# Gate chunks of the filler matmuls as seven block products (Strassen's scheme on 2x2 blocks), with the block sums on GpSimd

## The reference, cut to what matters

```
h = adaLN(RMSNorm(x))
(qa, ka, va, qb, kb, vb, zb, ab, bb, qc, kc, vc, ga, gb, gc) = split_cols(h @ w_in)
merged = sigmoid(ga) * (oa @ w_br_a) + sigmoid(gb) * (ob @ w_br_b) + sigmoid(gc) * (oc @ w_br_c)
x = x + gt1 * (merged @ w_out)
x = x + gt2 * expert_choice_ffn(adaLN(RMSNorm(x)))
```

## Time and profile before

| what | value |
|---|---|
| median of 3 runs | 3084.47 us (3082.32 to 3089.09) |
| the profiled execution's own time | 3082.67 us |
| span in the profile | 3080.9 us |
| TensorE busy | 3016.1 us, 98% of the span |
| VectorE, ScalarE, GpSimd busy | 1239.3, 605.8, 233.9 us |
| weights and stores moved | 695.55 MB |

### The profile page before, as it was taken

The page is one execution under the profiler, slowest core; times in us unless marked ns, Lnnn a source line. Parts: engine busy times, 40 slices in busy tenths (PEclk is TensorE's granted clock), DMA queues, the critical chain, the costliest instruction groups (busy, mean ns, idle before and its releaser), DMA issues.

```text
span 3080.9 us, 49607 instructions
## 1 busy us (share of the span) xinstructions
PE 3016.1 (98%) x21914; PEld 1605.2 (52%) x21914; DVE 1239.3 (40%) x2404; ACT 605.8 (20%) x1349; POOL 233.9 (8%) x374
## 2 busy tenths in 40 slices
PE   7999999999999999999999999999999999999998
PEld 3555565656556444444455546666565464444443
DVE  4459553364354121221254694533644342122113
ACT  3241001144423000000032400011534230000001
POOL 0011000021001000000100100000110010000000
PEclk9999999999999999999999999999999999999999
DMA  7235442432343999999941552434224349999997
GB/s 273 93 132 194 150 150 93 146 116 74 133 157 126 386 396 400 404 396 399 378 188 55 184 197 97 151 117 145 93 74 146 141 158 408 397 404 396 397 403 285
DMA packets 102294, 695.55 MB, mean 226 GB/s; under 512 B 11786, under 2 KB 25142, under 8 KB 66752
## 3 DMA queue, kind: packets, MB, share of 16 engines
q1 hardware_dynamic: 75296, 613.97, 50.6%
q0 software_dynamic: 20736, 62.80, 7.1%
q10 hardware_dynamic: 6048, 15.62, 1.3%
HBM read 618.66 MB, written 73.68 MB: 225 GB/s over the span
## 4 chain that ended last, share of the span: by engine, by line
PE 85%; DMA 11%; ACT 2%; DVE 1%; issue 0%; DVEq 0%; ACTq 0%
PE unit L997 14%; PE unit L951 12%; PE unit L1525 11%; DMA xT<-in_w_e_gate 9%; PE work L1528 8%; PE work L1525 5%; PE unit L1009 4%; PE unit L988 4%; PE unit L1028 4%; PE unit L1381 4%; PE unit L941 3%; PE work L965 1%; PE work L1171 1%; PE work L1194 1%; PE unit L1025 1%; PE unit L1393 1%
## 5 line engine op out<-in xcount | busy, mean ns | idle before, releaser
L997 PE MATMUL unit<-hT,ring 128*128 128x512 f32 x1024 | 452.6, 594 | 0.0
L997 PEld LDWEIGHTS unit<-hT,ring 128*128 128x128 f32 x1024 | 189.4, 190 | 217.7 <-issue 217.7
L2558 DVE SCALAR_TENSOR_TENSOR arena<-work,arena 32x256 f32<-32x256 f32 x128 | 61.7, 482 | 543.1 <-PE work L1528 541.7
L1525 PE MATMUL unit<-ring,arena 128*32 128x512 f32 x2112 | 238.8, 592 | 1.3 <-DVE arena L2546 1.3
L951 PE MATMUL unit<-hT,ring 128*128 128x512 f32 x512 | 222.2, 592 | 0.0
L1528 PE MATMUL work<-ring,arena 128*32 128x256 f32 x3072 | 183.8, 380 | 0.4 <-DVE arena L2546 0.4
L2028 ACT ACTIVATE arena<-work 128x512 f32<-128x512 f32 x32 | 19.1, 597 | 821.3 <-PE work L1543 821.3
L1635 ACT ACTIVATE xT<-unit 128x512 f32<-128x512 f32 x92 | 54.8, 596 | 590.6 <-PE unit L997 384.8
L951 PE MATMUL unit<-arena,ring 128*128 128x512 f32 x384 | 167.9, 593 | 1.6 <-ACT arena L1635 0.9
L951 PEld LDWEIGHTS unit<-hT,ring 128*128 128x128 f32 x512 | 96.2, 190 | 115.8 <-issue 115.5
L1528 PEld LDWEIGHTS work<-ring,arena 128*32 128x32 f32 x3072 | 97.3, 110 | 90.4 <-issue 37.8
(11 more groups left out here) (450 smaller groups left out, 4212.5 us busy)
## 6 DMA issues: line engine op xcount, KB each, us to landing
ring<-in_w_e_up SPq DMA_DIRECT2D x64, 2048.0 KB, 25.0
ring<-in_w_in SPq DMA_DIRECT2D x32, 2048.0 KB, 12.6
arena<-in_w_e_gate SPq DMA_DIRECT2D x32, 2048.0 KB, 24.4
arena<-in_w_e_down SPq DMA_DIRECT2D x32, 2048.0 KB, 26.0
xT<-in_w_e_gate SPq DMA_DIRECT2D x30, 2048.0 KB, 26.0
ring<-in_w_e_down SPq DMA_DIRECT2D x30, 2048.0 KB, 26.4
ring<-in_w_ada SPq DMA_DIRECT2D x24, 2048.0 KB, 9.5
spill<-xT SPq DMA_DIRECT2D x94, 256.0 KB, 9.6
```

The source lines that it names most:

```text
L997: last = mm(bank[:, :], w[:, k, m * P:(m + 1) * P], hT[:, k, 0:TS], start=k == 0, stop=k == KD - 1)
L1525: last = mm(big[SLOTP * c:SLOTP * c + SLOTP, :], x[:, s0:s0 + SLOTP], w[:, kk, 512 * (c // 2):512 * (c // 2) + 512], start=k == 0, stop=k ...
L2558: STT(y[SLS:SLS + SLOTP, 256 * c:256 * c + 256], W[5][r, 0:256], gpro[r, e:e + 1], gatep[r, :], ALU.mult, ALU.mult)
```

## The change

The four gate chunks of each layer are no longer computed as 5 units. Each is cut into two pairs; pair g covers output tiles m and m + 2 of 128 columns each (m = g mod 2), the contraction is cut into two halves of 4 k-tiles, and the 640 tokens into two halves of 320. That makes a product of 2x2 blocks, and it is done in Winograd's form of Strassen's scheme: seven block products r = 0 to 6 of 4 matmuls of 128x320 each instead of eight. The block sums are 15 additions: S1 to S4 of weights (4 per pair, 128x512), T1 to T4 of h (once per layer, 128x1280), and U2, U3, C11, C12 (two steps), C22, C21 of results (7 per pair, 128x320). GpSimd does all of them (`fast_sums`), in the order of `TASKS`, interleaved by hand with its DMA issues. S3, S4 overwrite the weights in the ring, and T1 overwrites a part of hT, which is saved to DRAM (`h_spill`) at the layer's start and brought back before attention. T2 to T4 take ring slot 2, so the gate chunks use slots 1, 0, 1, 0. ACT copies each product out of PSUM (`copy_fast`), and SP stores a finished pair (`store_pair`).

The order of the fills changes too: kc moves behind ka, ada 8 and 9 stand together, ada 10 and 11 stand together, and the steps of a group have 8, 7, 7, 7, 8, 8 calls. A call is now a credit: a matmul of 128x320 costs 5 of 8.

```
-UNITS_OF = dict(ada=0, fm=5, tm=5, br=5, late=0)
+UNITS_OF = dict(ada=0, fm=5, tm=5, br=5, late=0, fast=14)
 LATE = [("gc", 0), ("gc", 1)]
 BRANCHES = "bca"
-FILL = []
-_a = 4
-for _s in [("va", 0), ("kc", 0), ("qc", 0), ("vc", 0), ("qa", 0), ("ka", 0)] + [("g" + b, i) for b in "ab" for i in (0, 1)]:
-    if _a < 12:
-        FILL += [("ada", _a), _s] + [("fold", _a)] * (_a % 4 == 3)
-        _a += 1
-    else:
-        FILL += [_s]
+FAST = [("ga", 0), ("ga", 1), ("gb", 0), ("gb", 1)]
+FILL = [("ada", 4), ("va", 0), ("ada", 5), ("qc", 0), ("ada", 6), ("vc", 0), ("ada", 7), ("fold", 7), ("qa", 0), ("ada", 8),
+        ("ada", 9), ("ka", 0), ("ada", 10), ("ada", 11), ("kc", 0), ("fold", 11)] + FAST
 SPILLED = [_f for _f in FILL if _f[0] not in ("ada", "fold")]
+PLAIN = [_f for _f in SPILLED if _f not in FAST]
...
-MSLOTS = (0, 3, 1, 2, 4, 5)
+FIRST_FAST = PLAN.index(FAST[0])
+FIRST_LATE = PLAN.index(LATE[0])
+PRE_SLOTS = [q % RING for q in range(FIRST_FAST + 1)] + [0, 1, 0, 1, 2] + [q % RING for q in range(PRE_CHUNKS - FIRST_LATE - 2)]
+SUMS_SLOT = 2
+assert PRE_SLOTS[FIRST_FAST - 1:FIRST_FAST + 1] == [0, 1] and len(PRE_SLOTS) == PRE_CHUNKS
+MSLOTS = (2, 3, 0, 1, 4, 5)
 MRING = len(MSLOTS)
-assert PRE_CHUNKS % RING == 0 and NMOE % MRING == 0
+assert NMOE % MRING == 0
...
-STEPS = (9, 8, 8, 8, 8, 8)
+STEPS = (8, 7, 7, 7, 8, 8)
 GAPS = {("kv", 3): 3, ("kv", 4): 3} | {("pp", _t): 11 for _t in range(5)} | {"inverse": 90}
 GAPS |= {(_i, _j): _q for _i in range(5) for _j, _q in enumerate(STEPS)}
 GAPS |= {("o", _h): 8 if _h == 4 else 3 for _h in (4, 0, 1, 2, 3)}
 
 
+PIECE = dict(fast=5)
...
+        elif kind_of(name) == "fast":
+            units += [(name, i, j, 4, 5) for j in range(14)]
...
+def fast_tasks(units):
+    out = []
+    for name, i, j in units:
+        if (name, i) == PLAIN[-1] and j == 2:
+            out += [("t3", 0), ("t2", 0), ("t4", 0), ("s1", 0), ("s2", 0), ("s3", 0)]
+        if (name, i) == PLAIN[-1] and j == 4:
+            out += [("t1", 0)]
+        if kind_of(name) == "fast":
+            g, r = 2 * FAST.index((name, i)) + j // 7, j % 7
+            if r == 1:
+                out += [("s4", g)]
+            if r == 2:
+                out += [("u2", g), ("c11", g)]
+            if r == 3 and g + 1 < NPAIRS:
+                out += [("s1", g + 1), ("s2", g + 1), ("s3", g + 1)]
+            if r == 4:
+                out += [("u3", g)]
+            if r == 5:
+                out += [("c12a", g), ("c12", g), ("c22", g)]
+            if r == 6:
+                out += [("c21", g)]
+    return out
...
+        sets = [xflat[:, 4 * TH * i:4 * TH * i + 4 * TH] for i in range(2)]
+        tu2, tu3 = [xflat[:, 8 * TH + TH * i:8 * TH + TH * i + TH] for i in range(2)]
+        tp2 = xflat[:, 512 * 8 - TH:512 * 8]
+        S1 = rot.rearrange("p (k m) -> p k m", k=4)
+        S2 = xflat[:, 512 * 7 - TH:512 * 8 - TH].rearrange("p (k m) -> p k m", k=4)
+        T2, T3, T4 = [ring[SUMS_SLOT][:, 4 * TH * i:4 * TH * i + 4 * TH].rearrange("p (k t) -> p k t", k=4) for i in range(3)]
+        B11, B12 = [hT[:, 0:4, TH * i:TH * i + TH] for i in range(2)]
+        B21, B22 = [hT[:, 4:8, TH * i:TH * i + TH] for i in range(2)]
...
+                def store_pair(g):
+                    name, i = FAST[g // 2]
+                    to = spill[l, SPILLED.index((name, i))].rearrange("p (h t) -> p h t", h=H)
+                    sp.wait_ge(sig["summed"], task_done(l, "c21", g))
+                    sp.dma_start(to[:, g % 2:H:2, :], sets[g % 2].rearrange("p (a t) -> p a t", a=2))\
+                        .then_inc(sig[f"stage{g % 2}_stored"], 16)
...
+                sp.wait_ge(sig["h_ready"], (l + 1) * 2 * KD)
+                hsave = hspill[l].rearrange("p (k t) -> p k t", k=4)
+                sp.dma_start(hsave, B12).then_inc(sig["x_moved"], 16)
                 last = PLAN.index(SPILLED[-1])
-                for q in range(8, last + 3):
+                for q in range(8, FIRST_FAST + 1):
                     load_plan(q)
                     store_plan(q - 3)
+                store_plan(FIRST_FAST - 1)
+                load_plan(FIRST_FAST + 1)
+                for g in range(2 * len(FAST) - 2):
+                    if g % 2:
+                        load_plan(FIRST_FAST + 2 + g // 2)
+                    store_pair(g)
...
-                store_plan(last)
+                store_pair(NPAIRS - 2)
+                sp.wait_ge(sig["unit_computed"], fast_unit(l, NPAIRS - 1, 3) + 1)
+                sp.dma_start(B12, hsave).then_inc(sig["h_restored"], 16)
+                load_plan(FIRST_LATE + 1)
+                store_pair(NPAIRS - 1)
...
+                        if kind == "t3":
+                            pool.wait_ge(sig["h_ready"], 2 * KD * (l + 1))
+                            name, value = chunk_used(chunk_no(l, "ada", 11))
+                            pool.wait_ge(sig[name], value)
+                            add(T3, B22, B12, ALU.subtract, kind)
+                        elif kind == "t2":
+                            add(T2, T3, B11, ALU.add, kind)
+                        elif kind == "t4":
+                            add(T4, B21, T2, ALU.subtract, kind)
+                        elif kind == "t1":
+                            pool.wait_ge(sig["unit_computed"], unit_no(l, *PLAIN[-1]) + 5)
+                            pool.wait_ge(sig["x_moved"], 16 * (3 * l + 2))
+                            add(B12, B12, B11, ALU.subtract, kind)
+                        elif kind == "s1":
+                            pool.wait_ge(sig[f"chunk{slot}_loaded"], 16 * n)
+                            if g:
+                                pool.wait_ge(sig["unit_computed"], fast_unit(l, g - 1, 3) + 1)
+                            else:
+                                pool.wait_ge(sig["rotated"], len(ROTATED) * (l + 1))
+                            add(S1, A21, A22, ALU.add, kind)
+                        elif kind == "s2":
+                            if g:
+                                pool.wait_ge(sig["unit_computed"], fast_unit(l, g - 1, 2) + 1)
+                            else:
+                                pool.wait_ge(sig["rotated_stored"], 16 * len(ROTATED) * (l + 1))
+                            add(S2, S1, A11, ALU.subtract, kind)
+                        elif kind == "s3":
+                            add(A21, A11, A21, ALU.subtract, kind)
+                        elif kind == "s4":
+                            pool.wait_ge(sig["unit_computed"], fast_unit(l, g, 1) + 1)
+                            add(A12, A12, S2, ALU.subtract, kind)
+                        elif kind == "u2":
+                            pool.wait_ge(sig["unit_emptied"], fast_unit(l, g, 2) + 1)
+                            add(tu2, tu2, out[:, 0:TH], ALU.add, kind)
+                        elif kind == "c11":
+                            add(out[:, 0:TH], out[:, 0:TH], tp2, ALU.add, kind)
+                        elif kind == "u3":
+                            pool.wait_ge(sig["unit_emptied"], fast_unit(l, g, 4) + 1)
+                            add(tu3, tu3, tu2, ALU.add, kind)
+                        elif kind == "c12a":
+                            pool.wait_ge(sig["unit_emptied"], fast_unit(l, g, 5) + 1)
+                            add(out[:, TH:2 * TH], out[:, TH:2 * TH], tu2, ALU.add, kind)
+                        elif kind == "c12":
+                            add(out[:, TH:2 * TH], out[:, TH:2 * TH], out[:, 3 * TH:], ALU.add, kind)
+                        elif kind == "c22":
+                            add(out[:, 3 * TH:], out[:, 3 * TH:], tu3, ALU.add, kind)
+                        elif kind == "c21":
+                            pool.wait_ge(sig["unit_emptied"], fast_unit(l, g, 6) + 1)
+                            add(out[:, 2 * TH:3 * TH], out[:, 2 * TH:3 * TH], tu3, ALU.add, kind)
...
+            def fill_fast(l, name, i):
+                w = chunk_in(chunk_no(l, name, i))
+                for j in range(2):
+                    g = 2 * FAST.index((name, i)) + j
+                    A11, A12 = w[:, 0:4, tile_t(j)], w[:, 4:8, tile_t(j)]
+                    A21, A22 = w[:, 0:4, tile_t(j + 2)], w[:, 4:8, tile_t(j + 2)]
+                    for r, (x, y, need) in enumerate((
+                            (A11, B11, None), (A12, B21, None), (S2, T2, "s2"), (S1, B12, "s1"), (A21, T3, "s3"), (A12, B22, "s4"),
+                            (A22, T4, None))):
+                        n = unit_no(l, name, i, 7 * j + r)
+                        bank = begin(n)
+                        if need:
+                            pe.wait_ge(sig["summed"], task_done(l, need, g))
+                        if g == 0 and r == 3:
+                            pe.wait_ge(sig["summed"], task_done(l, "t1", 0))
+                        for k in range(4):
+                            last = mm(bank[:, 0:TH], x[:, k, :], y[:, k, :], start=k == 0, stop=k == 3)
+                            if k == 3:
+                                used(last)
```

(82 more changed lines are left out.)

89 lines of the change are left out of this document (58 added, 31 removed).

## The result

The change makes the kernel slower: 3101.14 us median (3099.79 to 3102.31, 5 runs) against 3085.96 us (3082.32 to 3089.09, 5 runs) of the kernel before, a ratio of 1.005 with a 95% interval of 1.0039 to 1.0062. The forecast was 3077 us with a range up to 3091, so the time lies outside the range and on the other side. The profiled execution took 3101.41 us, 18.7 us more than that of before (3082.67).

What follows compares the result with a forecast made beforehand. TensorE, busy 98%, was taken to bound the kernel. Matmuls -34.6, load waits +20.2 and low clock +6.6 sum to -7.8 us, from a median of 3084.47 to 3076.7, taken as 3077 us; range 3066 to 3091.

Steps and rivals of the forecast that it cites:

- What is removed, what is put in its place: Gate chunks: 276.9 us of matmuls replaced by 448 of 128x320 at 540.8 ns, 242.3 us; gain 34.6 us.
- Loads that the new order brings close: TensorE waits 4.5 us at ka and 5.5 at kc in each layer for their loads, 20.2 us in all.
- the four parallels: Four earlier ada loads with another load 2 us behind, landing after 9.0, 9.5, 8.7 and 9.4 us, mean 9.15.
- The clock after a wait: Clock falls to half after each of four load waits, 1.64 us each, 6.6 us in all; bounds 0 and 13.
- VectorE, and GpSimd's sums at nothing: DeltaNet groups: margins of about 4 us cover GpSimd's sums and VectorE's chain, so both cost nothing.
- The rest, at nothing: h_spill, attention's value load (about 2 us later), next layer's first ada load and ScalarE's copies all cost nothing.
- rival 2: Waits at ka and kc, but full clock after them: 3070 us; chance 14%.
- Rival 4: GpSimd's sums late, by themselves or by contention with VectorE: 4 to 12 us over the forecast, 3081 to 3089; 15%.
- Rival 3: ka's and kc's loads slowed by those issued behind them, landing after 13.6 us: +10.0, 3094 us; chance 8%.

Runs made afterwards that it cites:

- small sums in the mended kernel: Changed kernel with spread fill order, values loaded first, sums behind normalization and fold 7 apart, plus each GpSimd sum cut to one column: 3054.3 us, against 3055.19 with full sums.
- by the two runs: Changed kernel with each GpSimd sum on one column: 3095.95 us; changed kernel with four stage-end sums waiting for VectorE's normalization: 3093.64 us.
- by the run: Changed kernel with the value load issued ahead of gc's second chunk load and the last pair's store: 3092.03 us, 9.1 less than the change.

## Why the prediction was wrong, by its steps

**What is removed, what is put in its place: right.** 538 ns a matmul against 541 taken from the line; gain 35.7 against 34.6.

**Loads that the new order brings close: right in place, 2.4 us small.** 22.6 us against 20.2, at ka and kc in both layers. ka waits 5.1 to 5.3 us against 4.5, kc 6.0 to 6.1 against 5.5, the landings (9.7 and 9.6 us in layer 0, 9.5 and 9.5 in layer 1) being 0.3 to 0.5 us over the 9.15 that was taken. The trace of the kernel before holds two such ada loads that were not among the four parallels: issued at 229.88 and 348.46, with another load 3 to 4 us behind, they landed after 10.0 and 9.8 us. The run without the two loads and the run of the order alone both show this mechanism.

**The clock after a wait: right in kind, mis-sized.** 6.6 us were set for the four load waits; the stretches give 10.0. The price of a wait of 1 us was taken for one of 5 or 6. Here it was 1.8 to 3.1 us, so a wait cost nearly half again its length. It also fell behind waits that the prediction did not have (3.4). The Trainium skill (TensorE: Matmul & The Clock Gate, "What's actually happening") has the throttled clock as the default state, which activity releases. All four load waits agree with it; two waits of 2.8 us had the full clock behind them, so that sentence alone does not say which waits pay.

**VectorE, and GpSimd's sums at nothing: failed at one place.** The prediction costed contention in the gaps of the groups, found 4 us of margin there, and was right there: small sums in the mended kernel gain nothing. It did not look at the end of the stage, where TensorE stands still until VectorE's five products are done and where four sums fall at the same moment. 5.6 us of waits, and 5.2 to 7.5 by the two runs. The Trainium skill (GPSIMD Engine Reference, "Key points") says that GpSimd contends with VectorE instructions that have two SBUF inputs. VectorE's products here are of that kind, and the trace agrees: 0.62 us alone, 1.15 beside the sums.

**The rest, at nothing: failed.** The sentence "the value load of attention is now behind the last pair's store: about 2 us later than before" counted the store and left out the other thing the same queue had been given ahead of it, the 2 MB load of gc's second chunk. The values came 14.1 us after their issue, where the kernel before had them in under 7; 7.0 us of waits, 9.1 by the run. The next layer's first ada load was in time, as forecast (issued 18.5 us before its use, landed 4.7 before it).

So the terms that were set at nothing (5.6 + 7.0 + 3.4 = 16.0 us) are most of the error of 26.5 on the profiled execution (+18.7 against -7.8); the clock behind the loads gives 3.4, the loads 2.4, the matmuls -1.1, and the end of the experts -0.3. The other 6.1 us lie, as far as the rows show, where the change adds and moves no work, at a lower clock: the first projection of layer 0 ends 1.0 us later, that of layer 1 begins with 32 matmuls in 10.25 us against 8.85, and around the routers the mean clock is 0.93 (960 to 1012) and 0.91 (2495 to 2575) against 0.97 and 0.98 in the same work before. The number of falls there also differs between kernels that are alike there, and no run isolates it: what these 6.1 us come from stays open.

One slip in the prediction's range changes nothing: its low end of 3066 is said to be rival 2 with the better price of the matmuls, which gives 3068; 3066 needs the better landings too.

Rival 4 named the contention but at another place. Rival 3 had the sign and came nearest (3094), 7 us low, but by luck: its mechanism did not occur, since it needs landings of 12.8 us or more and ka's and kc's loads landed after 9.5 to 9.7.

## What to carry to other kernels

An order of work that makes room for something (here two chunks at the end, so that a slot is free for sums) is to be costed for every load in it: how long is what lies between the release of its slot and its use, against the landing time; the cure was another order, not a smaller change. When a load or store is put ahead of others on a queue, price each transfer that comes behind it by all the bytes now ahead of it. And look for contention where the slowed engine is the one that is waited for, not where it has the most work.

## What was not expected of the hardware

- A wait of 5 to 6 us cost TensorE 1.8 to 3.1 us more by a lower clock behind it, with TensorE busy throughout; two waits of 2.8 us, ended at 620.91 and 2191.34, had the full clock behind them (1.00), and a third of 2.8 us, at 2158.37, showed 1.7.
- One two-input VectorE instruction of 128x512 took 0.62 us alone and 1.15 beside GpSimd's sums, and GpSimd's sum of 128x320 took 0.92 alone and 1.27 beside it; five and four of them together took 5.76 us, less than the 6.78 of one group behind the other. Over the whole kernel the sums made VectorE busy for 31.7 us more, nearly all of it hidden.
- 1280 KB asked for 1.5 us after 2 MB, with a store of 640 KB between, all on the same queue, came after 15.3 us.
- A fall of the clock that does not happen need not be a gain: at the end of the experts 1.6 us were won by the full clock, and 1.3 of them went into a wait for a load whose issue did not move.
